# One change to a one-core hybrid encoder layer: modulation units spread over more steps, norm sums started one or two slots elsewhere and added over channel tiles in PSUM, the last expert combines merged

## The chip, the cores and the metric

One core of a Trainium2 chip runs the whole kernel. The metric is the device time of one execution in microseconds, taken as the median over runs.

## What is computed

One layer over 256 tokens of width 2048, float32 throughout, cut to what the change touches:

```python
mod = silu(c) @ w_ada[l] + b_ada[l]
shift1, scale1, gate1, shift2, scale2, gate2 = jnp.split(mod, 6, axis=-1)
h = modulate(rms_norm(x, norm1_g[l]), shift1, scale1)
p = h @ w_in[l]                     # 4096 columns: conv value, conv gate, ssm input, ssm gate
y_conv = conformer_conv(...)        # GLU, causal depthwise conv(31), LayerNorm over 1024 channels, silu
y_ssm = s5_ssm(...)                 # 64 groups of a 64-dim complex scan over the tokens, gelu, gate
y = jnp.concatenate([rms_norm(y_conv, ...), rms_norm(y_ssm, ...)], axis=-1) @ w_out[l]
x = x + gate1[:, None, :] * y
h = modulate(rms_norm(x, norm2_g[l]), shift2, scale2)
x = x + gate2[:, None, :] * hier_moe(h, ...)   # 32 SwiGLU experts, top-2 in one of 4 groups
return rms_norm(x, final_norm_g)
```

## The kernel before, in words

All weights, some 550 MB, stream through a ring of 12 buffers of 1 MB in on-chip memory. SyncE (SP) starts one transfer per buffer, in a fixed order, as soon as the buffer's last reader has signalled `consumed`; TensorE (PE) consumes the units in the same order. Each engine runs a list that is written out by hand, and all waits are on semaphores.

**Part A** (36 units). TensorE computes shift1 and scale1 with `column_unit` (lines 594 to 604): four matmuls of a unit put partial rows into a PSUM bank; after each fourth such unit ScalarE copies the bank to `modrow` (`column_copy(x)`, line 1201), TensorE folds that into columns (`columns(x)`, line 613) and VectorE adds and scales `hT`. The copies go in the order x = 0 to 7. In its list ScalarE has between them the three sine and absolute-value passes over tables of 4096 columns (lines 1239 to 1249) and the copies `keep_read` (line 1219) of turned state matrices. `columns(4)` stands in TensorE's list behind unit 21 and `columns(5)` behind unit 25; units 26 and 27 and the matmuls on `hT` (line 641) follow.

**Part B** (76 units, 28 steps g). Each step multiplies one unit of `w_in` with `hT` (`chunk_unit`, 16 matmuls 128x256, line 801); four steps make one chunk of 512 columns. The table `ada_in_step(g)` says how many units of `w_ada` (`ada_unit`, line 784) stand ahead of the chunk unit of step g. 16 of them make one part of the modulation vector (part 0 = gate1, part 1 = shift2, part 2 = scale2); the first unit of the next part waits until ScalarE has copied the part before it to `modrow` (`ada_copy`, line 1272), and that copy waits until GpSimd (POOL) has folded the part before that (`columns(n)` on GpSimd, lines 1473 to 1487), since there is one `modrow`. GpSimd's list is: eight `diagonal(q)` (line 1466, for the skip term of quad q), two `z_tiles` (line 1496, the GLU product), `mean_w`, then `columns(0)`, `columns(1)`, `columns(2)`.

Three slots belong to a step: 3g ahead of the chunk unit, 3g+1 in its middle, 3g+2 behind it. The tables `DRIVE_AT`, `READ_AT` and `SUM_AT` put side jobs at slots: a *drive* (line 834) gives VectorE the input of a quad of state pairs, a *read* (lines 848 and 851) turns its states into output, a *sum* (`channel_sum`, line 819) gives a norm its mean over 1024 channels. VectorE's list is quads 0 to 3, the convolution of the upper four tiles (`convolve(1, 0)`, 120 instructions of line 1751), quads 4 to 6, `convolve(0, 1)`, the norms of the convolution, and quad 7.

A norm's sum is made in two stages: VectorE adds the 8 channel tiles with one reduce (`add_tiles`, line 1760), and one matmul with a matrix of 1/1024 adds over the 128 partitions. There are four: the mean, the variance, the mean square of `y_conv`, and that of `y_ssm`. ScalarE squares the 8 tiles in one instruction ahead of each (lines 1298, 1309, 1328).

**Part C** (32 units): `out_units(m)` multiply with `w_out` (line 890), 8 matmuls 128x512 each. `out_units(0)` needs the normed convolution, `out_units(6)` the normed state output. The read of quad 7 stands behind `out_units([0, 1])`, the fourth sum behind `out_units([2, 3])`.

**Experts**: eight jobs of four experts, 48 units each. Behind the last job's `down` matmuls (line 1043) the results are weighted and added to the tokens: `combine_last` (line 1079) makes 16 products in PSUM, 8 of the first expert pair between the `down` matmuls of the second pair, 8 behind them, and VectorE adds each to `acc` (line 1974). The final RMS norm follows, first for tokens 0 to 127 (`t` = 0), then for the rest.

## Time and profile before

| | |
|---|---|
| median of 3 runs | 1532.99 us (1531.12 to 1535.0) |
| the profiled execution: its own time | 1533.17 us |
| its span, first to last instruction | 1531.4 us |
| TensorE busy | 1426.3 us (93%), granted clock 0.977 |
| VectorE, ScalarE, GpSimd busy | 554.0, 160.0, 158.9 us |
| moved by DMA | 565.45 MB, 369 GB/s over the span |
| chain that ended last | PE 62%, DVE 13%, DMA 8%, issue 6%, PEld 3%, POOL 3% |

The profile counts time from the start of the span. A matmul of float32 appears as two records, so x32 in the profile are 16 instructions. The busy time of a group is the time that it covers; the start of the next group tells how long it really held the engine. Part A ends at about 128 us, part B at about 421, part C at about 560; the experts follow.

### The profile page before, as it was taken

The numbers are of one execution on the slowest core, as the hardware profiler recorded it, in microseconds if no ns is written. First come the engines' busy times: TensorE is split into PE (matmuls) and PEld (weight loads), VectorE is DVE, ScalarE is ACT, GpSimd is POOL, SyncE is SP. The second block draws the span as 40 slices with busy tenths as digits, with TensorE's granted clock in tenths as the row PEclk, the third lists the DMA queues.
The fourth block names the chain that finished last, engine by engine and source line by source line (L and its number), as shares of the span: only waits on it lengthen the run. The fifth ranks groups of instructions, "written<-read, shape, count | busy, mean of one in ns | idle before, by whom it ended". The sixth has DMA issues, their size and how long they took to land.

```text
span 1531.4 us, 18660 instructions
## 1 busy us (share of the span) xinstructions
PE 1426.3 (93%) x7328; PEld 660.2 (43%) x7328; DVE 554.0 (36%) x950; ACT 160.0 (10%) x254; POOL 158.9 (10%) x112
## 2 busy tenths in 40 slices
PE   4989999996999979999999999999999999999977
PEld 2557777664544433333333343343343343333322
DVE  4235999996667430121121121121111111111105
ACT  3140100000411221000000010000010010000001
POOL 1000057067100035000000000000000000000000
PEclk9799999998999989999999999999999999999989
DMA  9999567599979949999999999999999999999992
GB/s 316 384 386 398 178 220 251 189 349 356 386 283 350 363 193 365 408 421 421 421 422 422 422 422 422 422 422 422 422 422 422 422 422 422 422 421 422 422 420 116
DMA packets 111008, 565.45 MB, mean 369 GB/s; under 512 B 10632, under 2 KB 10816, under 8 KB 52656
## 3 DMA queue, kind: packets, MB, share of 16 engines
q1 hardware_dynamic: 108368, 560.02, 91.0%
q10 hardware_dynamic: 2592, 4.78, 0.9%
q8 instruction: 32, 0.52, 0.1%
q14 instruction: 16, 0.13, 0.0%
HBM read 562.62 MB, written 2.13 MB: 369 GB/s over the span
## 4 chain that ended last, share of the span: by engine, by line
PE 62%; DVE 13%; DMA 8%; issue 6%; PEld 3%; POOL 3%; PEldq 2%; ACT 1%; SPq 1%; DVEq 0%; ACTq 0%; POOLq 0%
PE ps L1009 23%; PE ps L1043 15%; PE ps L977 8%; PE ps L1063 6%; DMA ring<-in_exp_w_down 6%; DVE arena L1751 3%; POOL skip L1466 3%; DVE arena L1721 2%; PEld ps L890 2%; PE ps L586 2%; PE ps L801 2%; DMA ring<-in_w_ada 1%; PEldq L894 1%; DVE arena L1709 1%; DVE arena L1708 1%
## 5 line engine op out<-in xcount | busy, mean ns | idle before, releaser
L1009 PE MATMUL ps<-ring,arena 128*64 128x512 f32 x2008 | 450.7, 593 | 7.4 <-DMA ring<-in_exp_w_up 4.7
L1009 PEld LDWEIGHTS ps<-ring,arena 128*64 128x64 f32 x2008 | 151.8, 137 | 276.5 <-issue 272.9
L1043 PE MATMUL ps<-ring,arena 128*64 128x512 f32 x1024 | 244.1, 603 | 19.8 <-issue 10.4
L801 PE MATMUL ps<-arena,ring 128*128 128x256 f32 x896 | 201.5, 382 | 1.3 <-ACT arena L1285 0.8
L801 PEld LDWEIGHTS ps<-arena,ring 128*128 128x128 f32 x896 | 167.8, 190 | 43.5 <-issue 21.9
L1974 DVE TENSOR_TENSOR arena<-arena,ps 128x512 f32<-128x512 f32 x72 | 49.5, 688 | 277.7 <-PE ps L1063 262.9
L1043 PEld LDWEIGHTS ps<-ring,arena 128*64 128x64 f32 x1024 | 72.0, 138 | 161.3 <-issue 152.9
L977 PE MATMUL ps<-arena 128*64 128x256 f32 x1024 | 124.6, 388 | 6.4 <-issue 3.8
L1466 POOL TENSOR_SCALAR skip<-ident,vT 128x128 f32<-128x128 f32 x8 | 97.7, 12218 | 209.5 <-PE ps L851 207.1
L1948 DVE TENSOR_SCALAR arena<-ps,mod 128x256 f32<-128x256 f32 x64 | 34.8, 544 | 228.1 <-PE ps L977 228.1
L890 PE MATMUL ps<-ring,arena 128*128 128x512 f32 x256 | 111.4, 594 | 1.4 <-ACT arena L1285 1.3
L1063 PE MATMUL ps<-arena 128*64 128x512 f32 x448 | 106.6, 595 | 2.9 <-issue 1.9
L977 PEld LDWEIGHTS ps<-arena 128*64 128x64 f32 x1024 | 74.0, 139 | 70.1 <-issue 42.8
L1751 DVE SCALAR_TENSOR_TENSOR arena<-arena 128x256 f32<-128x256 f32 x240 | 95.2, 477 | 0.0
L890 PEld LDWEIGHTS ps<-ring,arena 128*128 128x128 f32 x256 | 48.2, 190 | 61.1 <-issue 60.7
L1962 DVE TENSOR_TENSOR arena<-arena,ps 128x512 f32<-128x512 f32 x16 | 11.0, 687 | 173.7 <-PEq L1015 172.5
L1955 DVE TENSOR_TENSOR arena<-ps,arena 128x512 f32<-128x512 f32 x64 | 44.3, 692 | 61.6 <-PEq L1049 61.6
L1383 ACT ACTIVATE arena<-ps,mod 128x256 f32<-128x256 f32 x64 | 36.1, 564 | 279.9 <-PE ps L977 279.9
L1063 PEld LDWEIGHTS ps<-arena 128*64 128x64 f32 x448 | 32.0, 137 | 70.1 <-issue 70.1
L784 PE MATMUL ps<-ring,ccol 128*32 128x512 f32 x384 | 47.6, 615 | 12.0 <-ACT modrow L1272 11.5
L602 PE MATMUL ps<-ring,ccol 128*32 128x512 f32 x256 | 40.6, 755 | 19.1 <-DMA ring<-in_w_ada 19.0
L586 PEld LDWEIGHTS ps<-ident,arena 128*128 128x128 f32 (+3 forms) x276 | 31.9, 162 | 38.1 <-issue 35.3
(268 smaller groups left out, 746.3 us busy)
## 6 DMA issues: line engine op xcount, KB each, us to landing
ring<-in_exp_w_down SPq DMA_DIRECT2D x128, 1024.0 KB, 20.5
ring<-in_exp_w_gate SPq DMA_DIRECT2D x127, 1024.0 KB, 18.3
ring<-in_exp_w_up SPq DMA_DIRECT2D x124, 1024.0 KB, 17.0
ring<-in_w_ada SPq DMA_DIRECT2D x96, 1024.0 KB, 11.6
ring<-in_w_in SPq DMA_DIRECT2D x32, 1024.0 KB, 12.2
ring<-in_w_out SPq DMA_DIRECT2D x16, 1024.0 KB, 9.8
arena<-in_exp_w_up SPq DMA_DIRECT2D x4, 1024.0 KB, 11.1
arena<-in_x SPq DMA_DIRECT2D x2, 1024.0 KB, 7.1
```

The costliest lines, as they stand in the source:

```text
L586: return nc.tensor.transpose(dst, src, ident[0:k, 0:k])
L784: last = mm(ps[32 * j:32 * j + 32, 2, :], ccol[:, k:k + 1].to_broadcast([P, 32]), ring[:, s, j * N:(j + 1) * N], start=(k == 0), stop=(k = ...
L801: last = mm(ps[:, j // 2, (j % 2) * T:(j % 2 + 1) * T], ring[:, s, kk * N + j * P:kk * N + (j + 1) * P], hT[:, k, :], start=(k == 0 and j ...
L890: last = mm(ps[:, OUT_BANKS[c][t], :], src[:, k0 + kk, t * P:(t + 1) * P], ring[:, s, kk * N:(kk + 1) * N], start=first, stop=end, skip_gr ...
L977: last = mm(ps[half, 6 + k % 2, 0:T], x1p[:, t, k, half], pick[:, t, :], start=(t == 0), stop=(t == 1), skip_group_check=True)
L1009: last = mm(ps[64 * x:64 * x + 64, stage, :], xT[:, k, slot:slot + SLOTS], unit[:, kk * N:(kk + 1) * N], start=(k == 0), stop=(k == KD - 1 ...
L1043: last = mm(ps[half, 2 + n, :], hidT[pr][:, u, half], job_unit(m + x, False)[:, n * N:(n + 1) * N], start=(u == 0), stop=(u == 3), skip_gr ...
L1063: last = mm(ps[64 * x:64 * x + 64, 6 + t, :], wpickT[:, pr, t * P + 64 * x:t * P + 64 * x + 64], yexp[pr][:, n, :], start=(pr == 0), stop= ...
L1466: gp_.tensor_scalar(skip[:, :], ident[:, :], vT[:, 4, q:q + 1], None, ALU.mult).then_inc(skip_ready, 1)
L1751: ins = V.scalar_tensor_tensor(conv[:, c, :], z, cwT[:, c, j:j + 1], conv[:, c, :], ALU.mult, ALU.add)
L1955: V.tensor_tensor(yexp[pr][:, n, :], ps[:, 2 + n, :], gate2[:, n * N:(n + 1) * N], ALU.mult).then_inc(down_stored, 1)
L1974: V.tensor_tensor(acc[:, t, cc], acc[:, t, cc], ps[:, bank, :], ALU.add).then_inc(added, 1)
```

## The change

Four edits:

- **Modulation units**: steps 0 to 15 get one unit of `w_ada` each (before: every second of the steps 0 to 7, and each of the steps 8 to 19), steps 16 to 19 none. Part 0 is then complete in step 15 and no more in step 19. GpSimd's `columns(0)` moves from behind `diagonal(7)` to between `diagonal(4)` and `diagonal(5)`.
- **Tables in part A**: ScalarE makes `column_copy(4)` and `keep_read(7)` ahead of the table passes, and `column_copy(5)` behind them.
- **Sums**: VectorE's four reduces go. TensorE takes the 8 channel tiles one after another and adds them in PSUM, 8 matmuls a sum in the place of 1. ScalarE squares in two halves, and the matmuls of a half wait for that half. The second sum moves from slot 76 to 77, the third from 80 to 82, and the last read from behind `out_units([0, 1])` to behind `out_units([0, 1, 2])`.
- **Last combines**: both expert pairs are added in PSUM, 4 matmuls a product, 8 products in the place of 16, all behind the last `down`; VectorE adds 8 times in the place of 16.

```diff
-    if g < 8:
-        return g % 2
-    return 1 if g < 20 else 4
+    if g < 16:
+        return 1
+    return 0 if g < 20 else 4
...
 DRIVE_AT = [1, 3, 9, 15, 37, 44, 50, 55]
-READ_AT = [8, 14, 20, 26, 49, 55, 60, 85]
-SUM_AT = [74, 76, 80]
+READ_AT = [8, 14, 20, 26, 49, 55, 60, 86]
+SUM_AT = [74, 77, 82]
...
                 pe.wait_ge(sum_consts, 1)
-                pe.wait_ge(reduced, n + 1)
+                if n == 0:
+                    pe.wait_ge(conv_step, CT_ * TAPS)
                 if n < 3:
...
                     pe.wait_ge(drive_read, QUADS)
-                mm(ps[:, 3 if n < 3 else 7, 0:T], mean_w, csum, start=True, stop=True).then_inc(sums, 1)
+                for c in range(CT_):
+                    if n and c % 4 == 0:
+                        pe.wait_ge(squares, 2 * (n - 1) + c // 4 + 1)
+                    last = mm(ps[:, 3 if n < 3 else 7, 0:T], mean_w, (sq if n else conv)[:, c, :], start=(c == 0), stop=(c == CT_ - 1))
+                last.then_inc(sums, 1)
...
-            out_units([0, 1])
-            side(85)
-            out_units([2, 3])
+            out_units([0, 1, 2])
+            side(86)
+            out_units([3])
             channel_sum(3)
...
-                pr, m = divmod(i, 8)
-                n, t = divmod(m, 2) if pr == 0 else (m % 4, m // 4)
+                t, n = divmod(i, 4)
                 if i == 0:
                     pe.wait_ge(scatter_ready, j + 1)
-                if pr == 0 and t == 0 or pr == 1 and t == 0:
-                    pe.wait_ge(down_stored, j * 8 + 4 * pr + n + 1)
+                if t == 0:
+                    pe.wait_ge(down_stored, j * 8 + 4 + n + 1)
                 if i >= 2:
                     pe.wait_ge(added, j * 8 + i - 1)
-                for x in range(2):
-                    mm(ps[64 * x:64 * x + 64, 6 + i % 2, :], wpickT[:, pr, t * P + 64 * x:t * P + 64 * x + 64],
-                       yexp[pr][:, n, :], start=True, stop=True, skip_group_check=True).then_inc(combined, 1)
+                for pr in range(2):
+                    for x in range(2):
+                        last = mm(ps[64 * x:64 * x + 64, 6 + i % 2, :], wpickT[:, pr, t * P + 64 * x:t * P + 64 * x + 64],
+                                  yexp[pr][:, n, :], start=(pr == 0), stop=(pr == 1), skip_group_check=True)
+                        if pr == 1:
+                            last.then_inc(combined, 1)
...
                     turn_hidden(j_last, 1)
-                for m in {4: range(0, 3), 5: range(3, 6), 6: range(6, 8)}.get(i, ()):
-                    combine_last(j_last, m)
-            for m in range(8, 16):
-                combine_last(j_last, m)
+            for i in range(8):
+                combine_last(j_last, i)
...
                 keep_read(r)
+            column_copy(4)
+            keep_read(7)
             act.wait_ge(phase_ready, 1)
...
             A(rot128[:, 1, :], rot128[:, 0, :], ACT.Sin, scale=TWO_PI_DOWN).then_inc(table_sin, 1)
-            column_copy(4)
-            keep_read(7)
             act.wait_ge(table_sin, 2)
...
             A(rot128[:, 0, :], rot128[:, 0, :], ACT.Abs).then_inc(table_abs, 1)
-            column_copy(5)
             act.wait_ge(table_abs, 2)
...
             nc.scalar.copy(wr, wr_early).then_inc(wr_ready, 1)
+            column_copy(5)
             column_copy(6)
...
+            def square_tiles(v):
+
+                for h in range(2):
+                    c = slice(4 * h, 4 * h + 4)
+                    A(sq[:, c, :], v[:, c, :], ACT.Square).then_inc(squares, 1)
+
             def side(slot):
...
                             act.wait_ge(centred, 1)
-                            A(sq, conv, ACT.Square).then_inc(squares, 1)
+                            square_tiles(conv)
                         else:
...
                             act.wait_ge(swished, CT_)
-                            A(sq, conv, ACT.Square).then_inc(squares, 1)
+                            square_tiles(conv)
...
                     act.dma_start(col(gate_dram[0]), mod[:, 2, :]).then_inc(gate_stored, 16)
-            side(85)
+            side(86)
...
             act.wait_ge(gated, 1)
-            A(sq, uT, ACT.Square).then_inc(squares, 1)
+            square_tiles(uT)
...
                 t, n = divmod(i, 4)
-                act.wait_ge(added, j_last * 8 + 8 + i + 1)
+                act.wait_ge(added, j_last * 8 + i + 1)
                 if i:
...
             diagonal(4)
+            columns(0)
             diagonal(5)
...
             gp_.memset(mean_w, 1.0 / CH).then_inc(sum_consts, 1)
-            columns(0)
             columns(1)
...
-            def add_tiles(v):
-
-                V.tensor_reduce(csum, v.rearrange("p c t -> p t c"), AX.X, ALU.add).then_inc(reduced, 1)
-
-
             def centre():
...
-            def add_squares(n):
-                dve.wait_ge(squares, n)
-                dve.wait_ge(sums, n)
-                add_tiles(sq)
-
             def scale_conv():
...
             convolve(0, 1)
-            dve.wait_ge(sum_consts, 1)
-            dve.wait_ge(conv_step, CT_ * TAPS)
-            add_tiles(conv)
             centre()
-            add_squares(1)
             scale_conv()
-            add_squares(2)
             norm_conv()
...
             V.tensor_tensor(uT, uT, sgT, ALU.mult).then_inc(gated, 1)
-            dve.wait_ge(squares, 3)
-            add_tiles(sq)
             dve.wait_ge(sum_kept, 4)
...
             store_down(j_last, 0)
-            for i in range(8):
-                add(j_last, i, i // 2, i % 2, 6 + i % 2)
-            dve.wait_ge(added, j_last * 8 + 8)
             store_down(j_last, 1)
             for i in range(8):
-                add(j_last, 8 + i, i % 4, i // 4, 6 + i % 2)
+                add(j_last, i, i % 4, i // 4, 6 + i % 2)
                 if i == 5:
...
             dve.wait_ge(gain_landed, 16)
-            dve.wait_ge(added, j_last * 8 + 16)
+            dve.wait_ge(added, j_last * 8 + 8)
             final_rows(0)
```

How the lists now read. **ScalarE in part A**, from the end of `keep_read(6)`; L1201 (in the change L1204) is `column_copy`, and L1219 (L1222) `keep_read`. Before:

```order
L1239 ACTIVATE arena<-arena 128x4096 [waits table_phase_ready]
L1240 ACTIVATE rot<-rot 128x32
L1201 COPY modrow<-ps 128x512 [waits mod_column_block_done,ada_part_done]
L1219 COPY arena<-ps 64x32x2x4 [waits b_blocks_zeroed,b_c_blocks_turned]
L1219 COPY arena<-ps 64x32x2x4
L1244 ACTIVATE arena<-arena 128x4096 [waits table_sin_done]
L1245 ACTIVATE rot<-rot 128x32
L1201 COPY modrow<-ps 128x512 [waits mod_column_block_done,ada_part_done]
L1248 ACTIVATE arena<-arena 128x4096 [waits table_abs_done]
```

and of the change:

```order
L1204 COPY modrow<-ps 128x512 [waits mod_column_block_done,ada_part_done]
L1222 COPY arena<-ps 64x32x2x4 [waits b_blocks_zeroed,b_c_blocks_turned]
L1222 COPY arena<-ps 64x32x2x4
L1244 ACT_TABLE_LOAD
L1244 ACTIVATE arena<-arena 128x4096 [waits table_phase_ready]
L1245 ACTIVATE rot<-rot 128x32
L1247 ACTIVATE arena<-arena 128x4096 [waits table_sin_done]
L1248 ACTIVATE rot<-rot 128x32
L1250 ACTIVATE arena<-arena 128x4096 [waits table_abs_done]
L1251 ACTIVATE rot<-rot,arena 128x32
L1253 COPY arena<-arena 128x576 [waits router_weights_staged]
L1204 COPY modrow<-ps 128x512 [waits mod_column_block_done,ada_part_done] x2
```

`column_copy(4)` has moved ahead of the three long passes, and `column_copy(5)`, which stood ahead of the third, now stands behind it and behind the copy of the router weights.

**GpSimd in part B**: L1466 (L1475) is `diagonal`, L1496 (L1505) `z_tiles`, the first `modrow` row `columns`. Before:

```order
L1496 TENSOR_TENSOR arena<-arena 128x4x256 [waits chunk_bank_stored]
L1466 TENSOR_SCALAR skip<-ident,vT 128x128 [waits side_bank_done] x3
L1496 TENSOR_TENSOR arena<-arena 128x4x256 [waits chunk_bank_stored]
L1466 TENSOR_SCALAR skip<-ident,vT 128x128 [waits side_bank_done]
L1507 MEMSET arena 128x128 [waits z_tiles_ready]
L1473 TENSOR_TENSOR modrow<-modrow,own 128x512 [waits ada_part_copied]
L1476 TENSOR_TENSOR modrow<-modrow 128x256 [waits pool_order]
```

and of the change:

```order
L1505 TENSOR_TENSOR arena<-arena 128x4x256 [waits chunk_bank_stored]
L1475 TENSOR_SCALAR skip<-ident,vT 128x128 [waits side_bank_done]
L1482 TENSOR_TENSOR modrow<-modrow,own 128x512 [waits ada_part_copied]
L1485 TENSOR_TENSOR modrow<-modrow 128x256 [waits pool_order]
L1485 TENSOR_TENSOR modrow<-modrow 128x128 [waits pool_order]
L1485 TENSOR_TENSOR modrow<-modrow 128x64 [waits pool_order]
L1485 TENSOR_TENSOR modrow<-modrow 128x32 [waits pool_order]
L1488 TENSOR_TENSOR mod<-modrow 128x16 [waits pool_order]
L1491 TENSOR_TENSOR mod<-mod,bada 128x16 [waits late_setup_landed,mod_columns_ready]
L1475 TENSOR_SCALAR skip<-ident,vT 128x128 [waits side_bank_done] x2
L1505 TENSOR_TENSOR arena<-arena 128x4x256 [waits chunk_bank_stored]
L1475 TENSOR_SCALAR skip<-ident,vT 128x128 [waits side_bank_done]
```

The seven instructions of `columns(0)` stand ahead of two diagonals, the second `z_tiles` and the last diagonal.

**TensorE around the second sum** (step 25 and the first unit of step 26): L784 (L782) are modulation units, L801 (L799) the chunk unit, L819 (L821) the sum. Before:

```order
L784 MATMUL ps<-ring,ccol 32x512 x3
L801 MATMUL ps<-arena,ring 128x256 [waits unit_landed_5]
L801 MATMUL ps<-arena,ring 128x256 x7
L819 MATMUL ps<-arena 128x256 [waits side_bank_stored,sums_kept,tiles_added,sum_constants_ready]
L801 MATMUL ps<-arena,ring 128x256 x8
L784 MATMUL ps<-ring,ccol 32x512 [waits unit_landed_6]
```

and of the change:

```order
L782 MATMUL ps<-ring,ccol 32x512 x3
L799 MATMUL ps<-arena,ring 128x256 [waits unit_landed_5]
L799 MATMUL ps<-arena,ring 128x256 x15
L821 MATMUL ps<-arena 128x256 [waits sums_kept,squares_ready,side_bank_stored,sum_constants_ready]
L821 MATMUL ps<-arena 128x256 x3
L821 MATMUL ps<-arena 128x256 [waits squares_ready]
L821 MATMUL ps<-arena 128x256 x3
L782 MATMUL ps<-ring,ccol 32x512 [waits unit_landed_6]
```

One matmul in the middle of the chunk unit has become eight behind it, and the wait for VectorE's reduce a wait for ScalarE's squares.

## Rows read from the trace of the kernel before

**Rows 1.** The page, part 2: traffic in the 40 slices of 38.3 us
```profile
GB/s 316 384 386 398 178 220 251 189 349 356 386 283 350 363 193 365 408 421 421 421 422 422 422 422 422 422 422 422 422 422 422 422 422 422 422 421 422 422 420 116
```
**Rows 2.** Chain of waits, 120 to 560 us: start us, length us, what
```profile
321.25 46.39 POOL skip L1466
...
384.23 0.43 PE ps L819 x2
```
**Rows 3.** Timeline of TensorE, 300 to 440 us: start, busy us, count, idle before
```profile
338.82 3.64 PE L784 MATMUL ps<-ring,ccol 128*32 128x512 f32 x32
342.39 7.17 PE L801 MATMUL ps<-arena,ring 128*128 128x256 f32 x32
...
353.27 7.17 PE L801 MATMUL ps<-arena,ring 128*128 128x256 f32 x32
371.90 5.22 PE L784 MATMUL ps<-ring,ccol 128*32 128x512 f32 x32 [11.46 <-ACT modrow L1272]
...
421.06 13.97 PE L890 MATMUL ps<-ring,arena 128*128 128x512 f32 x32 [1.27 <-ACT arena L1285]
```
**Rows 4.** Timeline of ScalarE, 0 to 122 us
```profile
85.98 1.28 ACT L1239 ACT_TABLE_LOAD   x1
88.77 3.62 ACT L1239 ACTIVATE arena<-arena 128x4096 f32<-128x4096 f32 x1 [1.51 <-DVE rot L1686]
...
93.80 3.62 ACT L1244 ACTIVATE arena<-arena 128x4096 f32<-128x4096 f32 x1
...
100.54 0.59 ACT L1201 COPY modrow<-ps 128x512 f32<-128x512 f32 x1 [3.01 <-PEq L606]
101.02 3.71 ACT L1248 ACTIVATE arena<-arena 128x4096 f32<-128x4096 f32 x1
...
104.85 0.66 ACT L1251 COPY arena<-arena 128x576 f32<-128x576 f32 x1
```
**Rows 5.** Timeline of TensorE, 60 to 130 us
```profile
85.09 1.92 PE L602 MATMUL ps<-ring,ccol 128*32 128x512 f32 x16
...
93.17 1.87 PE L613 MATMUL ps<-arena,modrow 128*128 128x1 f32 x8 [5.37 <-ACT modrow L1201]
94.97 5.45 PE L602 MATMUL ps<-ring,ccol 128*32 128x512 f32 x32
101.18 1.05 PE L613 MATMUL ps<-arena,modrow 128*128 128x1 f32 x8 [0.76 <-ACT modrow L1201]
```
**Rows 6.** Stretches of 2 us: engines busy, clock, DMA share, GB/s
```profile
98.00:100.00 2.00, 2.00 (x20) 0.44 (x12) 0.00 (x0) 0.00 (x0) 0.00 (x0) 0.83 1.06 388
374.00:376.00 2.00, 2.00 (x16) 0.44 (x12) 0.00 (x0) 0.25 (x1) 1.34 (x5) 0.71 0.55 123
```
**Rows 7.** Timeline of VectorE, 120 to 460 us
```profile
143.90 3.11 DVE L1721 TENSOR_TENSOR_SCAN arena<-decay,carry,arena 128x128 f32<-128x128 f32 x8
...
200.35 4.98 DVE L1721 TENSOR_TENSOR_SCAN arena<-decay,carry,arena 128x128 f32<-128x128 f32 x8
...
415.70 2.28 DVE L1708 TENSOR_TENSOR arena<-ps,arena 128x2048 f32<-128x2048 f32 x1
```
**Rows 8.** Timeline of GpSimd, the whole span
```profile
202.81 2.24 POOL L1496 TENSOR_TENSOR arena<-arena 128x1024 f32<-128x1024 f32 x1 [8.48 <-ACT arena L1285]
...
367.75 1.06 POOL L1473 TENSOR_TENSOR modrow<-modrow,own 128x512 f32<-128x512 f32 x1
368.88 1.99 POOL L1476 TENSOR_TENSOR modrow<-modrow 128x256 f32<-128x256 f32 x4
```
**Rows 9.** Timeline of TensorE, 120 to 440 us
```profile
301.62 1.15 PE L834 MATMUL ps<-arena 32*128 32x256 f32 x16 [1.22 <-DVE arena L1709]
```
**Rows 10.** Timeline of ScalarE, 100 to 560 us
```profile
408.96 0.47 ACT L1302 ACTIVATE arena<-ps,arena 128x256 f32<-128x256 f32 x1 [3.22 <-PE ps L819]
```
**Rows 11.** Timeline of TensorE, 1440 to 1532 us
```profile
1513.53 7.62 PE L1079 MATMUL ps<-arena 128*64 128x512 f32 x32 [0.27 <-issue]
```
**Rows 12.** Stretch of 2 us at the end of the weight stream
```profile
1498.00:1500.00 2.00, 2.00 (x12) 0.72 (x9) 0.32 (x1) 0.00 (x0) 0.00 (x0) 1.00 0.37 147
```

More of the change, by code:

```diff
@@ L170, in trunk @@
         mean_w = at(116, P)
-        csum = at(117, T)
         x1sq = at(24, N)
@@ L343, in trunk @@
         squares = sem("squares_ready")
-        reduced = sem("tiles_added")
         sums = sem("sums_done")
```

## The prediction

> **What bounds the kernel now.** I read the page's traffic first. From slice 16 to the last but one it stands at 408 to 422 GB/s [rows 1]: from about 615 us the weight stream of the experts bounds the kernel, and it begins as early as TensorE gets there. So whatever moves TensorE's arrival at the experts moves the end by as much, and only three places can matter: part A, parts B and C, and the tail behind the last weights. The chain of waits names the largest single piece ahead of the experts: 46.39 us of one GpSimd instruction, `diagonal(7)` [rows 2]. It began at 321.25, when VectorE had begun `convolve(0, 1)`, and ended with it. `columns(0)` was queued behind it, the copy of part 1 waited for `columns(0)`, and TensorE stood for 11.46 us ahead of the first unit of part 2 [rows 3]. That unit's group then took 5.22 us where the one before took 3.64 [rows 3], since the granted clock had fallen to the lower of its two levels, 1.2 GHz, during the stand, and was back at 2.4 only inside 374 to 376 [rows 6].
>
> **Part A, the tables.** The last units ahead of `column_copy(4)` end at 87.0 [rows 5]. Now that copy and `keep_read(7)` come first; with the short sine they fill the 1.4 us between the first long pass and the second [rows 4], so they end at about 88.5. The table load, 1.28, ran in idle time before; now it follows, and the first pass starts at 89.8 and not at 88.77 [rows 4]. The passes then follow each other at 3.8 each, and the third with the router copy takes 4.5 (101.02 to 105.5): end at 101.9. Only then comes `column_copy(5)`, 0.59, until 102.5; before it was done at 101.1 [rows 4]. TensorE gets `columns(4)` at 87.8 in place of 93.17, and does units 22 to 25 at the full clock in 3.84 (twice the 1.92 of 16 records) instead of 5.45 [rows 5]. But then it stands from 92.5 to 102.5 for `column_copy(5)`. It gains nothing by its early start: **+1.4 us**. And it restarts at the lower level. After 5.37 us of standing the clock returned inside 98 to 100, 5.5 us after the restart; after 11.46 us, 3.3 us after it [rows 3, 5, 6]. At half the clock that loses 1.6 to 2.8; I take 2.1. Part A ends 3.5 us later, between 3.0 and 4.2.
>
> **Part B up to the stall.** VectorE works without a gap from quad 0 to quad 6, and TensorE waits for it at the last drive, 1.22 us [rows 9]. So the units that move (four more up to step 7, three fewer in steps 16 to 18) count only where VectorE waits for them. The unit now ahead of step 0 delays quad 0 by 0.9 (3.64 for four units [rows 3]), and the one that step 19 loses behind that wait gives 0.9 back: nothing. Their transfers move with them; SP's queue keeps its order and runs as far ahead as the ring lets it. What counts is `columns(0)`. ScalarE copies part 0 in step 15, about 272 with the delay, and GpSimd then works while VectorE is in the scans of quad 4. At the same pair in quad 3, `z_tiles` held GpSimd for 2.24 us and eight scans took 4.98 in place of 3.11 [rows 7, 8], so VectorE lost 1.87, 83% of it. `columns(0)` takes 3.5 (from 367.75 until the copy that ends at 371.90 could start [rows 3, 8]), so **+2.9 us**, on the path because VectorE is. The bounds are nothing (GpSimd works in gaps) and 3.5. The other way round GpSimd gave way for all of a convolution [rows 2], but the new place is not in one. The Trainium skill, page "SBUF — State Buffer", section "Who interferes with whom", says that whoever issues first gets the shared port pair for the whole instruction and the other fully blocks; by that VectorE would lose all of GpSimd's time, 3.5 us, and the sum would be 0.6 higher. The scan that began as `z_tiles` ran agrees; 46.39 us for one `diagonal`, behind a hundred VectorE instructions, does not.
>
> **From the stall to the fourth sum.** Chunk unit 23 ends at 360.4 (353.27 and 7.1) [rows 3], in its own time; part 1 can be copied at once, as `columns(0)` is long done, and the stand of 11.46 and the 1.6 of the low clock go. What is late next are the sums. A record of 128x256 costs 0.222 (7.1 for 32 [rows 3]), so a sum of eight matmuls costs 3.55 where one cost 0.43 [rows 2]: 3.1 more, four times. VectorE's reduces go from the waits between. Steps 24 to 27 are 10.67 each (338.82, then 3.57 to 342.39, then 7.1 [rows 3]). TensorE is through the third sum, which stands in the middle of step 27, at 360.4 + 42.7 - 3.55 + 3 x 3.55 = 410.2. From there root, reciprocal and eight scalings are as before: from 408.96 to 415.70 is 6.7 [rows 7, 10]. They end at 417.0. TensorE has the chunk done at 413.8 and waits 3.2 for them; that is the new stall. Part C starts at 417.1, and not at 421.06 [rows 3]: 4.0 earlier. The fourth sum takes 3.1 of that back, the later read I cost at nothing: unit 3 of `w_out` lies between it and the fourth sum, 7.0 us (13.97 for two [rows 3]), and covers gelu, gate and squares, an estimate of 5; without that cover TensorE would wait for the rest. SP, which waits for that read ahead of loading x again, starts this some 3 us later, and only the residual behind the fourth sum reads it. **-0.9 us**, between -2 and +0.5.
>
> **Tail.** The combines between the `down` matmuls leave: 32 records, and the last `down` starts some 7.5 us earlier. The weights are all there: traffic drops inside 1498 to 1500 [rows 12], while that `down` would begin at about 1501. But the final products now are 64 records and not 32, which took 7.62 [rows 11]. TensorE's work is the same. What is won is that the root of the first 128 tokens is taken while products still run, some 0.5: **-0.5 us**, between -1.9 (records at the 0.215 of the `down` groups, an estimate) and +0.3. VectorE's eight adds fewer are hidden under TensorE.
>
> **Sum**: 3.5 + 2.9 - 0.9 - 0.5 = +5.0 us. The profiled execution took 1533.17 us, 1.8 more than its span, and the median is 1532.99, so I put it on either: 1538.0.
>
> **Rivals.**
> *GpSimd costs VectorE nothing* and the clock comes back at the early bound: +2.1 or less, 1533.5 to 1535.1. For it: GpSimd's pieces of `columns` are short, with waits between them. Against: the scan of rows 7. It decides at 2.5 us less than my sum. 22%. This is the case that is not slower.
> *Neither early shift reaches the stall*, because TensorE's restart in A and VectorE's loss lie beside something that I take for free: 1531.6. Against it: VectorE has no gap. 15%.
> *The sums are cheap*: matmuls with the same stationary matrix follow at less than 0.22. With half of it, four sums give back 7, and alone that makes 1531; with the first rival too, about 1528 or less. Against it: 0.43 for the two records of a sum [rows 2], no faster than others. With what I overlook on this side, 15%.
> *The ring runs dry*: steps 20 to 27 use five units in 10.67, and the stream needs about 2.6 us a unit, 13. The stand let it catch up; without it TensorE has 12 units in store at step 20 and loses some 2 in 10.67 us, over eight steps with 10 us of sums between. By that it keeps some units in hand; if not, TensorE waits up to 5 us in steps 26 and 27: 1543. 8%.
>
> **The numbers.** My own case has 40%: 1535.5 to 1541. Not more, since it rests on two small delays whose size I take from one place each. A measurement tells this kernel from another at about 0.3%, 4.6 us: slower is above 1537.6, faster below 1528.4. My case falls on both sides of the upper line, the first two rivals within. Slower 0.40, same 0.43, faster 0.17. The range 1529.5 to 1541.5 leaves out about one in ten on each side.
>
> **What would show it.** In A: TensorE's idle time ahead of the `columns(5)` matmul of 10 us, part B from about 132. In B: scans of quad 4 of over 2 us beside GpSimd; no idle time ahead of the first unit of part 2, at about 367. In C: sums of 3.5 us, some 3 us of waiting for ScalarE or VectorE ahead of line 893. In the tail: the last product ending as late behind the last `down`'s end as 15 us. It would be wrong if part B began at 128 or earlier, if the sums took under 3 us, or if part C began more than 3 us before 421.

## The result, and the profile after

The changed kernel takes 1536.39 us (median of 16 runs, 1534.15 to 1538.58), the kernel before 1531.58 in the same comparison: ratio 1.0026, 95% interval 1.0019 to 1.0033. The two medians are 4.8 us apart; the ratio itself, taken over all runs, says 4.0, with 2.9 to 5.1 as its interval. The forecast was 1538.0, 5.0 above the 1533.0 of before. The profiled execution of the changed kernel took 1535.92 us with a span of 1534.1, which is 2.75 above the profiled execution of before. The ledger below adds up to that smaller difference: the profiled execution of before lies 1.6 above its kernel's median of this comparison, that of the changed kernel 0.5 below its own.

The page of the changed kernel, busy times, traffic by slices of 38.4 us, and the chain that ended last:

```profile
PE 1435.1 (94%) x7384; PEld 672.0 (44%) x7384; DVE 534.3 (35%) x938; ACT 160.4 (10%) x257; POOL 160.4 (10%) x112
...
GB/s 319 384 388 401 225 228 263 138 268 416 401 259 327 361 217 335 408 421 421 421 421 423 421 422 422 421 423 421 423 421 422 422 422 423 421 422 421 423 421 129
...
PE 66%; DVE 12%; DMA 8%; issue 6%; PEld 4%; PEldq 1%; ACT 1%; SPq 1%; DVEq 0%; ACTq 0%
```

GpSimd's 3% has left the chain (the 46 us of `diagonal(7)` [rows 2]), and TensorE's share went from 62 to 66%. Traffic is at 416 and 401 in slices 9 and 10 (counted from 0), where 356 and 386 stood [rows 1]: the stall's place is filled. From slice 16 to the last but one it differs by no more than 1 GB/s. TensorE's busy time rose by 8.8 us, VectorE's fell by 19.7.

**Part A.** TensorE, 60 to 134 us (start, busy, count, idle before), then stretches with the columns PE, PEld, DVE, ACT, POOL busy, granted clock (1.00 is 2.4 GHz, 0.50 is 1.2), DMA share, GB/s:

```profile
83.26 1.92 PE L600 MATMUL ps<-ring,ccol 128*32 128x512 f32 x16
...
100.76 1.87 PE L611 MATMUL ps<-arena,modrow 128*128 128x1 f32 x8 [10.20 <-ACT modrow L1204]
102.55 3.52 PE L600 MATMUL ps<-ring,ccol 128*32 128x512 f32 x16
...
123.08 8.74 PE L639 MATMUL ps<-arena,ring 128*128 128x256 f32 x32 [0.86 <-DVE arena L1661]
132.07 1.07 PE L782 MATMUL ps<-ring,ccol 128*32 128x512 f32 x8 [0.26 <-issue]
```

```profile
100.00:104.00 4.00, 3.24 (x16) 2.18 (x20) 1.23 (x5) 0.68 (x2) 0.00 (x0) 0.50 1.05 387
104.00:106.00 2.00, 2.00 (x12) 0.20 (x4) 0.31 (x1) 0.00 (x0) 0.00 (x0) 0.54 1.05 385
106.00:110.00 4.00, 4.00 (x23) 3.53 (x20) 0.00 (x0) 0.00 (x0) 0.00 (x0) 1.00 1.05 387
122.00:126.00 4.00, 3.13 (x9) 2.52 (x10) 1.80 (x6) 0.00 (x0) 0.00 (x0) 0.61 1.06 403
```

TensorE stands for 10.20 us ahead of the `columns(5)` matmul, where it stood 5.37 ahead of `columns(4)` [rows 5]. It restarts at 0.50, the 16 records behind it take 3.52 us instead of 1.92, and the clock is back at about 106. Part B begins at 132.07 and not at 128.33, 3.7 later. But the group of 83.26 began at 85.09 before [rows 5], and the last group of u took 8.74 for its 32 records, against 7.15 before. Both are short falls of the clock that only one of the two executions has at that place; more on this at the first experiment.

**Part B.** GpSimd in `columns(0)`, and VectorE's two runs of eight scans in quad 4:

```profile
271.78 1.08 POOL L1482 TENSOR_TENSOR modrow<-modrow,own 128x512 f32<-128x512 f32 x1 [7.12 <-ACT modrow L1275]
272.93 1.99 POOL L1485 TENSOR_TENSOR modrow<-modrow 128x256 f32<-128x256 f32 x4
```

```profile
271.26 4.25 DVE L1730 TENSOR_TENSOR_SCAN arena<-decay,arena 128x128 f32<-128x128 f32 x8
...
276.35 3.11 DVE L1730 TENSOR_TENSOR_SCAN arena<-decay,carry,arena 128x128 f32<-128x128 f32 x8
```

The first eight took 4.25 us. In quads without GpSimd beside them they take 2.63, so VectorE lost 1.62 of `columns(0)`'s 3.7 us. It lost them scan by scan: the one that starts at 271.92, beside GpSimd's first multiply, took 1.22 us, the next two, beside the adds, 0.88 and 0.61, where a scan of this kind without GpSimd takes 0.40.

**The stall, the sums and part C.** TensorE from 300 us, and VectorE around the third sum:

```profile
308.12 1.15 PE L837 MATMUL ps<-arena 32*128 32x256 f32 x16 [2.16 <-DVE arena L1718]
...
365.80 3.64 PE L782 MATMUL ps<-ring,ccol 128*32 128x512 f32 x32 [0.26 <-issue]
...
376.38 3.62 PE L821 MATMUL ps<-arena 128*128 128x256 f32 x16
...
412.06 3.62 PE L821 MATMUL ps<-arena 128*128 128x256 f32 x16
...
421.41 20.84 PE L893 MATMUL ps<-ring,arena 128*128 128x512 f32 x48 [2.28 <-DVE arena L1781]
...
451.44 3.62 PE L821 MATMUL ps<-arena 128*128 128x256 f32 x16
```

```profile
416.22 1.75 DVE L1779 RECIPROCAL arena<-arena 128x256 f32<-128x256 f32 x1 [17.47 <-ACT arena L1311]
418.01 3.26 DVE L1781 SCALAR_TENSOR_TENSOR arena<-arena,vT 128x256 f32<-128x256 f32 x8
```

The 11.46 us ahead of the first unit of part 2 are gone (0.26), and the unit takes 3.64 and not 5.22 [rows 3]. It starts 6.1 us earlier, in spite of the 5.1 that parts A and B had lost. Each sum now has 16 records and takes 3.6 us. At the line that begins part C nearly all is gone: 421.41 against 421.06 [rows 3], with 2.28 us of waiting for VectorE's scalings. Behind the fourth sum the kernel is 3.4 us later than before, measured from sum end to sum end.

**Tail.** TensorE in the last job:

```profile
1483.10 11.44 PE L1046 MATMUL ps<-ring,arena 128*64 128x512 f32 x48
1495.02 14.87 PE L1046 MATMUL ps<-ring,arena 128*64 128x512 f32 x64 [0.47 <-issue]
1510.26 13.95 PE L1082 MATMUL ps<-arena 128*64 128x512 f32 x64 [0.36 <-issue]
```

The products stand in one block of 64 records, 13.95 us, where 32 records took 7.62 behind the last `down` [rows 11]. From the start of the group of 48 `down` records (1479.18 before) to VectorE's last two outputs (1525.79 before, 1528.46 now) it was 46.61 us and is 45.36.

The ledger, profile against profile: part A +3.7, part B +1.4, stall with sums -1.7, from there to the last job +0.5, tail -1.2: **+2.7 us**.

### The profile page after: what moved, and what is told of

Read it like the earlier page. It is cut to its first block, busy times and chain, and to the rows that moved or that the text cites. A ratio compares the mean times of both kernels' runs of the same rounds, so it can differ in the third digit from the quotient of the medians.

```text
span 1534.1 us, 18744 instructions
## 1 busy us (share of the span) xinstructions
PE 1435.1 (94%) x7384; PEld 672.0 (44%) x7384; DVE 534.3 (35%) x938; ACT 160.4 (10%) x257; POOL 160.4 (10%) x112
## 4 chain that ended last, share of the span: by engine, by line
PE 66%; DVE 12%; DMA 8%; issue 6%; PEld 4%; PEldq 1%; ACT 1%; SPq 1%; DVEq 0%; ACTq 0%
PE ps L1012 23%; PE ps L1046 15%; PE ps L980 8%; PE ps L1066 6%; DMA ring<-in_exp_w_down 6%; PE ps L799 4%; DVE arena L1760 3%; PEld ps L893 3%; DVE arena L1730 2%; PE ps L782 2%; PE ps L584 2%; PE ps L639 2%; DMA ring<-in_w_ada 1%; PE ps L600 1%; PEldq L897 1%
## 5 line engine op out<-in xcount | busy, mean ns | idle before, releaser
L799 PE MATMUL ps<-arena,ring 128*128 128x256 f32 x896 | 201.5, 382 | 1.2 <-ACT arena L1288 0.8
L799 PEld LDWEIGHTS ps<-arena,ring 128*128 128x128 f32 x896 | 167.8, 190 | 43.3 <-issue 21.7
L1966 DVE TENSOR_TENSOR arena<-arena,ps 128x512 f32<-128x512 f32 x64 | 44.0, 687 | 271.4 <-PE ps L1066 262.9
L1475 POOL TENSOR_SCALAR skip<-ident,vT 128x128 f32<-128x128 f32 x8 | 98.8, 12351 | 204.1 <-PE ps L854 201.8
L1954 DVE TENSOR_TENSOR arena<-arena,ps 128x512 f32<-128x512 f32 x16 | 11.0, 688 | 174.1 <-PEq L1018 172.9
L600 PE MATMUL ps<-ring,ccol 128*32 128x512 f32 x256 | 39.1, 731 | 18.9 <-DMA ring<-in_w_ada 18.9
L1403 ACT COPY arena<-ps 128x512 f32<-128x512 f32 x16 | 9.4, 586 | 369.9 <-PE ps L584 369.9
## 6 DMA issues: line engine op xcount, KB each, us to landing
arena<-in_exp_w_up SPq DMA_DIRECT2D x4, 1024.0 KB, 10.3
```

The lines of the kernel that those rows point to most:

```text
L600: last = mm(ps[32 * j:32 * j + 32, bank, :], ccol[:, k:k + 1].to_broadcast([P, 32]), ring[:, s, j * N:(j + 1) * N], start=(i == 0), stop=( ...
L799: last = mm(ps[:, j // 2, (j % 2) * T:(j % 2 + 1) * T], ring[:, s, kk * N + j * P:kk * N + (j + 1) * P], hT[:, k, :], start=(k == 0 and j ...
L1475: gp_.tensor_scalar(skip[:, :], ident[:, :], vT[:, 4, q:q + 1], None, ALU.mult).then_inc(skip_ready, 1)
L1966: V.tensor_tensor(acc[:, t, cc], acc[:, t, cc], ps[:, bank, :], ALU.add).then_inc(added, 1)
```

## Experiments

Each was timed in rounds with the kernel before on the same chip. Ratios are to that kernel; before took 1532.2 us beside the first four, 1533.13 beside the next four, 1532.05 beside the last two.

### One part taken out of the change at a time

**e1, the tables in the old order**: in ScalarE's block,

```
-            column_copy(4)
-            keep_read(7)
             act.wait_ge(phase_ready, 1)
...
+            column_copy(4)
+            keep_read(7)
             act.wait_ge(table_sin, 2)
...
+            column_copy(5)
             act.wait_ge(table_abs, 2)
...
             nc.scalar.copy(wr, wr_early).then_inc(wr_ready, 1)
-            column_copy(5)
```

> The changed kernel with ScalarE's table passes back in the old order (column_copy(5) between the Abs passes and the last sine). The two traces put part B 3.7 us later with the new order, but in three pieces: a clock dip at 66 to 72 us that only the run before had (1.8), the copy behind the passes with the slow restart (about 3.9), and a dip inside 120 to 134 us that only the changed run had (1.6). Theory 1, the copy and the restart are the whole of it and the dips come and go by chance: 3.5 to 4 us less than the changed kernel, about 1532.6. Theory 2, the new order also spares the dip at 66 to 72: only about 2 less, 1534.5. Theory 3, nothing of part A reaches the end: 1536.4.

Measured 1533.42 us (1530.41 to 1535.59, 11 runs), ratio 1.0004 (0.9995 to 1.0013): 3.0 less than the changed kernel. TensorE in part A:

```profile
91.39 1.87 PE L611 MATMUL ps<-arena,modrow 128*128 128x1 f32 x8 [5.36 <-ACT modrow L1204]
...
99.27 1.05 PE L611 MATMUL ps<-arena,modrow 128*128 128x1 f32 x8 [0.76 <-ACT modrow L1204]
...
119.17 8.83 PE L639 MATMUL ps<-arena,ring 128*128 128x256 f32 x32 [0.86 <-DVE arena L1661]
128.26 1.06 PE L782 MATMUL ps<-ring,ccol 128*32 128x512 f32 x8 [0.26 <-issue]
```

Theory 1 holds by the traces; the medians' 3.0 lie between it and theory 2. The `columns(5)` matmul starts at 99.27 and not at 100.76, 1.5 us earlier. The 32 records of the u unit behind it start at 102.10 and not at 106.01, so the clock accounts for the other 2.4, and part B starts 3.8 earlier. The short fall of the clock in the last u group (8.83) is there as in the changed kernel, and none at 66 to 72, as in the changed kernel: neither belongs to the order of the tables. A further one in this execution (the drive at 304.29 took 1.61 us for its 16 records and not 1.15) is why its span is only 1.8 below that of the changed kernel. Such falls, of 1.6 us or so each, came at 66, 119 to 127 or 305 us in different executions; how much of the 4 us by which executions of one kernel differ they make up isn't known, since one execution of each was traced. The kernel before had one in its profiled execution, at 66, too.

**e2, units and `columns(0)` where they were**:

```
-    if g < 16:
-        return 1
-    return 0 if g < 20 else 4
+    if g < 8:
+        return g % 2
+    return 1 if g < 20 else 4
...
             diagonal(4)
-            columns(0)
             diagonal(5)
...
+            columns(0)
             columns(1)
```

> The changed kernel with the modulation units and columns(0) where they were. Theory 1, the stand ahead of part 2 comes back whole: 11.5 of standing and 1.6 of low clock come, and VectorE's losses to columns(0) (1.6) and the later convolution go: part 2's first unit ends 9.5 to 10 us later than in the changed kernel (365.8 there), and the end with it, about 1546. Theory 2, the longer stand is partly taken back by the sums behind it (the 2.3 us wait ahead of line 893 goes) or by a fuller ring: 7 us, 1543.5. Theory 3, the stall was of no consequence for the end: 1535.

Measured 1547.83 us (4 runs), ratio 1.0102 (1.0087 to 1.0118): 11.4 more than the changed kernel, above even the first theory. TensorE:

```profile
375.78 5.53 PE L782 MATMUL ps<-ring,ccol 128*32 128x512 f32 x32 [11.45 <-ACT modrow L1275]
...
433.28 22.54 PE L893 MATMUL ps<-ring,arena 128*128 128x512 f32 x48 [2.28 <-DVE arena L1781]
```

The stand is back to the hundredth: 11.45 us, and 5.53 for the unit at the low clock. The unit starts 9.98 later than in the changed kernel, as theory 1 said, but that theory left out the low clock behind its start, 1.89 us: part C starts 11.87 later (433.28 against 421.41), and all of it reaches the end. TensorE still waits as long for the scalings (2.28), so that wait does not hang on the stall. That 48 records took 22.54 us there, and 20.84 in the changed kernel, is one more short fall of the clock, at 434 to 438 us of this execution (mean granted clock 0.57).

**e3, the sums on VectorE again**:

```
+            def add_tiles(v):
+                V.tensor_reduce(csum, v.rearrange("p c t -> p t c"), AX.X, ALU.add).then_inc(reduced, 1)
...
-                for c in range(CT_):
-                    if n and c % 4 == 0:
-                        pe.wait_ge(squares, 2 * (n - 1) + c // 4 + 1)
-                    last = mm(ps[:, 3 if n < 3 else 7, 0:T], mean_w, (sq if n else conv)[:, c, :], start=(c == 0), stop=(c == CT_ - 1))
-                last.then_inc(sums, 1)
+                mm(ps[:, 3 if n < 3 else 7, 0:T], mean_w, csum, start=True, stop=True).then_inc(sums, 1)
```

with the three slots and the last read where they were before.

> The changed kernel with the channel sums as before: VectorE adds the tiles, TensorE has one matmul of 0.43 us for each sum, and the sums and the last read stand at their old places. Theory 1, TensorE's extra 3.1 us for each of four sums is what took back the gain of the stall: 4 x 3.1 = 12.5 less, less 1.6 of waiting for the reduces, plus part of the 2.3 wait ahead of line 893: 10 to 12 us less than the changed kernel, 1525. Theory 2, the ring runs short of weights once the sums no longer give the stream time (four of them are 12.5 us): only 5 to 7 less, 1530. Theory 3, VectorE's reduces (3.65 each) are on the path as much as TensorE's matmuls: no change, 1536.

Measured 1527.21 us (5 runs), ratio 0.996 (0.9947 to 0.9974): 9.2 less than the changed kernel, and 5.0 less than before. TensorE, with a row of the last job:

```profile
365.64 3.64 PE L784 MATMUL ps<-ring,ccol 128*32 128x512 f32 x32 [0.26 <-issue]
...
401.72 0.67 PE L819 MATMUL ps<-arena 128*128 128x256 f32 x2 [0.32 <-issue]
...
414.53 13.97 PE L890 MATMUL ps<-ring,arena 128*128 128x512 f32 x32 [1.27 <-ACT arena L1285]
...
444.57 0.59 PE L819 MATMUL ps<-arena 128*128 128x256 f32 x2
...
1496.69 4.57 PE L1043 MATMUL ps<-ring,arena 128*64 128x512 f32 x16 [1.22 <-DMA ring<-in_exp_w_down]
```

The first unit of part 2 starts as in the changed kernel (365.64), the third sum 10.3 us earlier (7.3 of them for its old slot), part C 6.9, and behind the fourth sum TensorE is 9.9 earlier. So the sums in PSUM took back nearly all that the stall had given. TensorE waits 1.07, 1.25 and 0.32 us ahead of the three sums of part B, and never for weights between them, so theory 2 falls. The 9.2 are a little less than theory 1 said: of the 9.9, 1.2 went at the very end, to a wait for the last `down` weights.

**e4, the last combines as before**, with their 16 adds:

```
                 if i == 0:
                     turn_hidden(j_last, 1)
-            for i in range(8):
-                combine_last(j_last, i)
+                for m in {4: range(0, 3), 5: range(3, 6), 6: range(6, 8)}.get(i, ()):
+                    combine_last(j_last, m)
+            for m in range(8, 16):
+                combine_last(j_last, m)
```

> The changed kernel with the last combines as before: 16 adds, half of the products between the last down matmuls. Theory 1, what the two traces show from the first down to the end: 1.3 to 1.4 us more, 1537.8. Theory 2, the merged combines win only the earlier root: 0.5 more, 1536.9. Theory 3, nothing: 1536.4.

Measured 1536.77 us (10 runs), ratio 1.0029 (1.002 to 1.0039): 0.4 more than the changed kernel, less than the spread of either. In the trace the stretch from the group of 48 `down` records to the last output is 46.60 us, as in the kernel before (46.61), against 45.36. The trace speaks for theory 1, the medians for theory 2; e6 and e9 come back to it.

### The parts put together from the kernel before

**e5, only units and `columns(0)`** (the edit of e2, forwards, on the kernel before).

> The kernel before with only part B of the change: the modulation units spread and columns(0) behind diagonal(4). Tables, sums and tail as before. Theory 1, the stand of 11.46 us and the 1.6 of the low clock go, VectorE loses 1.6 to columns(0), and the first sum then waits about 1 for VectorE's reduce: 10 to 11 less than before, 1521.5. Theory 2, something behind it caps the gain, as in e3_sums_on_vector, where TensorE waited 1.2 us for the last down weights: only 8 to 9 less, 1524. Theory 3, the parts do not add (sums in PSUM are needed to use the time): 5 or less, above 1527.

Measured 1522.5 us (1521.71 to 1523.35, 5 runs), ratio 0.9931 (0.9917 to 0.9944): 10.6 less than before. TensorE:

```profile
372.26 0.67 PE L819 MATMUL ps<-arena 128*128 128x256 f32 x2 [0.19 <-issue]
...
381.40 0.67 PE L819 MATMUL ps<-arena 128*128 128x256 f32 x2 [1.24 <-issue]
...
396.54 0.67 PE L819 MATMUL ps<-arena 128*128 128x256 f32 x2 [0.34 <-issue]
```

Theory 1: no stand, and TensorE idles 0.19, 1.24 and 0.34 us ahead of the three sums, behind VectorE's reduces. That is what the sums in PSUM can save, 1.8 us here; in e3 and e8, where the first of the three waits is 1.07 and 1.09, it is 2.6 and 2.7. They cost 3.1 us each.

**e6, e5 with the merged combines**: the diff of e4 turned round, on e5.

> e5_units_and_columns_alone with the last combines merged as in the change. Theory 1, the tail's gain is TensorE's and VectorE's own work and comes on top: 1.2 less than e5. Theory 2, once TensorE waits for the last down weights, the products that stood between the down matmuls filled that wait for nothing, and taken out from there they are paid for behind the last down: 0 less, or up to 1 more.

Measured 1522.03 us, ratio 0.993: 0.5 less than e5, inside the spread. TensorE in the last job:

```profile
1468.34 11.45 PE L1043 MATMUL ps<-ring,arena 128*64 128x512 f32 x48
1480.26 14.87 PE L1043 MATMUL ps<-ring,arena 128*64 128x512 f32 x64 [0.47 <-issue]
1495.65 13.95 PE L1079 MATMUL ps<-arena 128*64 128x512 f32 x64 [0.52 <-issue]
```

From 1468.34 to the last outputs at 1513.86 it is 45.52 us; in e5 that was 46.70. In this execution TensorE waited for no `down` weights.

With e6, e3 and the changed kernel there is a ladder of ratios, each step adding one part: before 1, units and `columns(0)` 0.9931, merged combines 0.9930, tables 0.9960, sums in PSUM 1.0026. At 1532 us these steps are -10.6, -0.2, +4.6 and +10.1 us. Most of these ratios have an interval of 2 us to either side, and they come from three comparisons, so a single step is known to about 3 us.

**e7, e6 with a third order of the tables**: `column_copy(4)` and `keep_read(7)` first,

```
             A(rot128[:, 1, :], rot128[:, 0, :], ACT.Sin, scale=TWO_PI_DOWN).then_inc(table_sin, 1)
+            column_copy(5)
             act.wait_ge(table_sin, 2)
```

> e6 with a third order of the tables: column_copy(4) and keep_read(7) ahead of the passes as in the change, column_copy(5) between the first and the second pass. Theory 1, TensorE stands for neither copy: the 5.4 us ahead of columns(4), the 0.8 ahead of columns(5) and the 1.6 of low clock that the old order has all go, part B starts at about 121 and not at 128.3, and the end moves by as much: 6 to 7 less than e6. Theory 2, the weight stream, which runs at 387 GB/s through all of part A, becomes the bound there: 3 less. Theory 3, the end of part A does not count for the end any more: 0.

Measured 1522.18 us, ratio 0.9925 (0.9912 to 0.9939): no different from e6. TensorE in part A:

```profile
92.91 1.33 PE L613 MATMUL ps<-arena,modrow 128*128 128x1 f32 x8 [1.92 <-ACT modrow L1201]
...
110.93 1.06 PE L602 MATMUL ps<-ring,ccol 128*32 128x512 f32 x8 [0.84 <-DMA ring<-in_w_ada]
113.85 1.84 PE L602 MATMUL ps<-ring,ccol 128*32 128x512 f32 x8 [1.86 <-DMA ring<-in_w_ada]
116.42 1.87 PE L613 MATMUL ps<-arena,modrow 128*128 128x1 f32 x8 [0.73 <-ACT modrow L1201]
119.15 9.66 PE L641 MATMUL ps<-arena,ring 128*128 128x256 f32 x32 [0.86 <-DVE arena L1652]
```

The two stands are gone, 1.92 us is left of them, and the `columns(5)` matmul starts at 92.91, where e6 has it at 98.83. Then TensorE waits 0.84 and 1.86 us for `w_ada` from the ring, the clock falls again (1.87 for eight records of `columns`, 9.66 for 32 of the u unit) and part B starts at 129.10, later than in e6 (126.14). Theory 2, and more than it said: from 86 to 130 us the stream, at 379 to 404 GB/s, was right behind TensorE's stands. This execution is the slowest of its five, 2.2 above their median, so the fall of the clock need not be in the others. The weights alone bound the gain all the same: the last of them came at 113.85, and at the full clock their 8 records (1.06 us) would have ended 1.2 us ahead of the same ones in e6 (116.07), an estimate from these two traces. Theory 3 does not fit e1, where 3.8 us of part A reached the stall.

### The stall by itself

**e8, one line moved in the kernel before**:

```
             diagonal(6)
+            columns(0)
             z_tiles(0)
             diagonal(7)
...
-            columns(0)
             columns(1)
```

> The kernel before with a single line moved: columns(0) between diagonal(6) and z_tiles(0), the modulation units where they were. Part 0 is copied at 307.5 there, and GpSimd is idle from 301 to 316. Theory 1, the stall is wholly the queue behind diagonal(7), and the spread units are not needed: the stand and the low clock go, VectorE loses 0 to 2 us beside columns(0), 10 to 12 less than before, 1521. Theory 2, columns(0) holds back z_tiles(0) and the last convolution by some 3 us, and the first sum waits for it: 8 less, 1524. Theory 3, the units have to be spread too: 3 or less.

Measured 1520.44 us (1519.99 to 1522.92, 5 runs), ratio 0.9921 (0.9907 to 0.9935): 12.7 less than before, and 2.1 less than e5, though the two intervals overlap. GpSimd in `columns(0)`, then TensorE's first unit of part 2:

```profile
307.11 1.06 POOL L1473 TENSOR_TENSOR modrow<-modrow,own 128x512 f32<-128x512 f32 x1 [7.05 <-ACT modrow L1272]
308.24 1.99 POOL L1476 TENSOR_TENSOR modrow<-modrow 128x256 f32<-128x256 f32 x4
```

```profile
359.61 3.64 PE L784 MATMUL ps<-ring,ccol 128*32 128x512 f32 x32 [0.26 <-issue]
```

Part 0 was copied at 307 already, without the units moved, and GpSimd sat idle until `z_tiles(0)`. `diagonal(7)` is held as before, but nothing that TensorE waits for is queued behind it. VectorE's second scans of quad 6 took 4.52 us and not 3.11, a loss of 1.41. Behind quad 6 VectorE waits for `z_tiles(0)` anyway (2.63 us before, 2.14 here), and this took 0.5 of the loss: from the first scan of quad 6 to the last convolution it is 15.17 us, and 14.24 before, so 0.9 was lost. Behind `diagonal(4)`, the place in e5, VectorE has no gap and lost all of its 1.62. The traces bear out that this place is better, by about the 2.1 of the medians: part C starts at 408.52 here and at 409.35 in e5, though this execution was 1.15 later at 65 us (the `columns` matmul there starts at 65.21, in e5 at 64.06), and each of the two has one short fall of the clock, of 1.7 and 1.6 us. How much of it comes from the place and how much from the units, which e5 moves too, was not taken apart.

**e9, e8 with the merged combines**: the same diff, on e8.

> e8_columns_move_alone with the last combines merged as in the change. Theory 1, the two are independent: 0.5 to 1.2 less than e8, about 1519.5. Theory 2, an earlier arrival makes TensorE wait for the last down weights, and the merge then gives nothing: 1520.5 or more.

Measured 1519.29 us (1518.92 to 1520.48, 5 runs), ratio 0.9915 (0.9902 to 0.9929), the lowest median of all, but 1.15 below e8, from another comparison, is again within what two such measurements can tell. A row of the last job shows why it is uncertain:

```profile
1489.93 4.57 PE L1043 MATMUL ps<-ring,arena 128*64 128x512 f32 x16 [1.03 <-DMA ring<-in_exp_w_down]
```

Here TensorE waited 1.03 us for the last `down` weights, and the stretch to the last output was 46.59 us, no shorter than without the merge. Over e3, e4, e6 and e9 the merge gave 1.2 us of the stretch when the weights were there and nothing when they were not.

**e10, `columns(0)` behind `z_tiles(0)`**, so that it runs into the last convolution:

```
             diagonal(6)
-            columns(0)
             z_tiles(0)
+            columns(0)
             diagonal(7)
```

> e8 with columns(0) one place later on GpSimd: behind z_tiles(0), so that it meets the last convolution, and ahead of diagonal(7). Theory 1, a GpSimd instruction that starts inside VectorE's run of 120 two-input instructions is held to the end of the run, whichever it is (45 to 47 us for both diagonals): one of the eight instructions of columns(0) takes some 45 us, part 1 waits for it, and a stand of 7 to 11 us is back ahead of part 2: 1530 to 1533. Theory 2, only diagonal is slow there, and the short instructions of columns(0) get through between VectorE's: no stand, 1521.

Measured 1520.93 us (4 runs), ratio 0.992 (0.9905 to 0.9935): no stand. Theory 1 falls: `columns(0)` was done 1 us into the run, and not held. VectorE paid for it in the four instructions ahead of the run (L1747), 2.81 us and not 1.38. GpSimd, and the convolution's 120 multiply-adds on VectorE:

```profile
319.75 0.28 POOL L1479 TENSOR_TENSOR mod<-modrow 128x16 f32<-128x16 f32 x1
...
320.41 1.12 POOL L1466 TENSOR_SCALAR skip<-ident,vT 128x128 f32<-128x128 f32 x1
...
352.34 15.69 POOL L1473 TENSOR_TENSOR modrow<-modrow,own 128x512 f32<-128x512 f32 x1 [30.66 <-ACT modrow L1272]
```

```profile
319.42 47.69 DVE L1751 SCALAR_TENSOR_TENSOR arena<-arena 128x256 f32<-128x256 f32 x120
```

`diagonal(7)`, which started 1 us into that run, took 1.12 us. In e8 the same instruction, 0.75 us into the same run, was held to its end:

```profile
320.16 47.32 POOL L1466 TENSOR_SCALAR skip<-ident,vT 128x128 f32<-128x128 f32 x1 [2.15 <-PE ps L851]
```

## Why the prediction was right, and where not

**Part A, +3.5 (3.0 to 4.2).** Right: 3.8 in the trace of e1 and 3.0 in its median; 4.6 in the ladder, where the ratios leave about 3 us open. The composition held too: 1.5 for the later copy against 1.4 forecast, 2.4 for the slow restart against 2.1. The absolute times in the list of what would show it (a stand from 92.5 to 102.5) were 1.8 late, since they started from an execution with a fall of the clock at 66.

**Part B, +2.9 (0 to 3.5).** The mechanism was right and the size wrong: the scans lost 1.62, not 2.9. The step that failed took 83% from `z_tiles` beside scans [rows 7, 8] and put it on `columns(0)`. `z_tiles` is one instruction of 2.24 us over 128x1024, and held one scan for 2.33; `columns(0)` is seven short ones, and costs VectorE 1.62 of 3.7, or 44%. The sign that was named, scans of over 2 us, did not show: the longest took 1.22. In both places the scan that ran beside one GpSimd instruction lost less than that instruction's time (1.87 of 2.24, 0.8 of 1.08), so many short ones cost less than their sum; that this is the reason for the smaller share fits the scans, and no run changed the number of instructions to show it. The unit ahead of step 0 and the one that step 19 loses did cancel, as forecast: the last drive is 6.5 us later than before (308.12 against 301.62), the unit behind it 5.1 (320.08 against 314.98). The Trainium skill, page "SBUF — State Buffer", section "Who interferes with whom", has whoever issues first keep the shared ports for the whole instruction and the other fully block; summed over GpSimd's time, as the prediction did, that would have been near 3.5, which it was not.

**Stall to fourth sum, -0.9 (-2 to +0.5).** Measured -1.7, inside the range, and its pieces as forecast: stand and low clock gone (e2: 11.45 us of standing back at once), sums of 3.55 us by their starts and ends, in the kernel's own frame (less the 5.1 lost by then) the third sum over at 410.4 against 410.2, part C begun at 416.3 against 417.1. The difference is the eight scalings: 3.26 us where I took the 4.45 of before. There GpSimd's `columns(2)` ran beside them, at 413.27; now it is over at 413.5, ahead of them at 418.01. So the wait ahead of line 893 is 2.28 and not 3.2. That moving the last read costs nothing was right.

**Tail, -0.5 (-1.9 to +0.3).** -1.2 in the trace, -0.4 to -1.15 in the medians. I counted TensorE's work as the same and only the earlier root as gained. The step that failed is this first one. The 64 records in one block are busy for 13.95 us, 0.218 each; the 64 of before were spread over 12, 12, 8 and 32 and were busy for 3.02 + 2.92 + 1.89 + 7.62 = 15.45. From the start of the 48 `down` records TensorE is through after 41.1 us and not 42.0, and from there to the last two outputs it is 4.25 and not 4.64: 0.9 of the 1.25 is TensorE's, 0.4 the earlier root. The term's lower bound, -1.9, had allowed for records of 0.215.

**Sum.** +5.0 forecast, +4.8 in the medians (+4.0 by the ratio), +2.7 in the traces. The agreement with the medians is better than the terms earn, and in part luck: against the ledger B was 1.5 too high, stall and tail together 1.5 not low enough, A 0.2 too low, and 0.5 between the fourth sum and the last job was not in it at all: together 2.3 less than forecast. The 1536.4 lie in the range of the own case (1535.5 to 1541), and below the 1537.6 that it took as the limit of what a measurement can tell. The two falls of the clock in the traces nearly cancel (1.8 in before, 1.6 in the changed kernel), so the 2.7 of the traces is the sum of the terms for these two executions, and the medians lie 2 further apart for reasons that no single trace shows.

**Rivals.** That GpSimd costs VectorE nothing was wrong (1.62, and 1.41 in e8). That neither shift reaches the stall was wrong: e1's 3.8 arrived whole at 304 us. The sums were not cheap, and the ring did not run dry at steps 26 and 27 (0.26 and less ahead of every unit there). The ring mattered elsewhere, in part A (e7) and at the last `down` weights (e3, e9).

What the prediction didn't say, though its own numbers held it: the single line that takes `columns(0)` from behind `diagonal(7)` is worth 12.7 us alone (e8), and the four sums in PSUM cost TensorE 12.4 to save it waits of 1.8 to 2.7.

## What to carry to other kernels

Where one engine bounds the stretch, work moved onto it from an idle engine costs its whole duration, and all that it can give back are the waits that the trace shows ahead of it: here 1.07, 1.25 and 0.32 us of waiting (e3) against three times 3.1. Look at a stall first for what is queued in front of the late instruction on its own engine, and move only that; then take the parts of a mixed change one by one, since a small net result can hold terms of -11 and +10. And ask of each stand that you remove what is right behind it, by timing the version without it: in part A it was the weight stream (e7).

## What the runs showed that was not expected

- A GpSimd instruction beside VectorE's run of 120 multiply-adds is held to the end of the run in one kernel and passes in another. In e8 `diagonal(7)` started at 320.16, 0.75 us into the run and after 2.15 us of idling for its semaphore, and took 47.32 us. In e10 it started at 320.41, 0.99 us into the run and straight behind the instructions of `columns(0)`, and took 1.12. In e10 again, the first multiply of `columns(1)` started at 352.34 after 30.66 us of idling and took 15.69, until the convolution was over at 367.1. Whether it is the idling or the semaphore wait ahead of it that decides was not tried.
- TensorE's clock falls for some 1.6 us of lost time in the middle of part A or B without a long stand ahead of it, at another place from execution to execution (66 us in the one of before and in e10; 118 to 128 in after, e1, e2, e3, e4, e8 and e9; 302 to 310 in e1, e5, e6 and e7; 434 in e2). And the `columns` matmul near 65 us starts anywhere from 64.06 (e5) to 66.28 (e7), behind a stretch from about 34 to 56 us in which every trace has the clock at or near its lower level for most of the time. A difference of 2 us between two traces means nothing until these are taken out.
- A wait for weights of only 1.86 us stood in a stretch with a mean clock of 0.63 (112 to 120 us in e7). The two groups behind it took 1.87 and 9.66 us where e6 has 1.05 and 7.14, 3.3 us more, so the clock cost more than the wait.
